# Differential attention as one pipeline over its heads, RWKV blocks inverted in 64x64 halves, and inverse roots by logarithm and exponential

## The reference, cut to what matters

```python
def _rmsnorm(x, g, eps=NORM_EPS):          # used on x, on the MLA latents, on the output of differential attention
    y = xf * lax.rsqrt(jnp.mean(xf * xf, axis=-1, keepdims=True) + eps)
    return (y * g.astype(jnp.float32)).astype(x.dtype)

def _rwkv7_mix(...):                       # 8 heads of 64
    kk = kk / jnp.maximum(jnp.linalg.norm(kk, axis=-1, keepdims=True), 1e-12)
    def step(state, inp):                  # 1024 steps
        sa = jnp.einsum('bhij,bhj->bhi', state, -kk_t)
        state = (state * w_t[:, :, None, :] + sa[..., None] * b_t[:, :, None, :]
                 + v_t[..., None] * k_t[:, :, None, :])
        return state, jnp.einsum('bhij,bhj->bhi', state, r_t)
    y = ((y - mean) * lax.rsqrt(var + RWKV_GN_EPS)).reshape(B, S, RWKV_DIM) * ln_w + ln_b

def _diff_mix(...):                        # 4 heads, two maps each, Q_BLOCK = 128
    def block(q0, q1, mask):
        logits = jnp.einsum('bhmqd,bhmkd->bhmqk', q[:, :, :, q0:q1], k[:, :, :, :q1]) * scale + bias
        probs = _masked_softmax(logits, mask)
        attn = probs[:, :, 0] - lam_full * probs[:, :, 1]
        return jnp.einsum('bhqk,bhkd->bhqd', attn.astype(v.dtype), v[:, :, :q1])
    o = _rmsnorm(o, subln, eps=1e-5) * (1 - lambda_init)
```

## Time and profile before

| what | value |
|---|---|
| median of 3 runs | 6106.19 us (6104.87 to 6108.89) |
| profiled execution | 6102.16 us, span 6100.4 us |
| PE, DVE, ACT, POOL busy | 85%, 31%, 22%, 10% of the span |
| mean granted clock of TensorE | 0.91 |
| one RWKV pair (the second) | 531.0 to 772.5 us |
| differential attention behind its projections | 2030.7 to 2306.1 us |

### The profile page before, as it was taken

How to read it: one execution, slowest core, us unless ns; L and a number is a source line. 1 busy time by engine, 2 the same in 40 slices (tenths; PEclk the granted TensorE clock), 3 DMA queues, 4 the chain that set the end, 5 groups by cost and what they waited for, 6 DMA issues and landing times. The chain is left out here.

```text
span 6100.4 us, 63978 instructions
## 1 busy us (share of the span) xinstructions
PE 5159.5 (85%) x24753; PEld 2840.6 (47%) x24753; DVE 1895.1 (31%) x3299; ACT 1331.5 (22%) x2074; POOL 616.5 (10%) x419
## 2 busy tenths in 40 slices
PE   6688888898799657799989949787788876999899
PEld 2264756743354344344434414675556642444344
DVE  5343442511640351211110034544423632111101
ACT  2222121211330351122220011223213421222200
POOL 0030220300000001000000010222210001000000
PEclk9898898889899768899999979898889998999999
DMA  3501001010011002111113302101110001111111
GB/s 76 84 6 27 18 20 28 6 47 26 11 36 49 31 31 83 32 38 38 40 47 102 111 11 68 38 5 41 41 39 1 1 21 28 38 38 38 36 38 50
DMA packets 301641, 231.72 MB, mean 38 GB/s; under 512 B 30355, under 2 KB 266695, under 8 KB 301383
## 3 DMA queue, kind: packets, MB, share of 16 engines
q1 hardware_dynamic: 301418, 228.46, 13.4%
HBM read 203.76 MB, written 24.67 MB: 37 GB/s over the span
## 5 line engine op out<-in xcount | busy, mean ns | idle before, releaser
L628 PE MATMUL psum<-ffn_in,up_slots 128*128 128x512 f32 x2816 | 1213.8, 594 | 65.3 <-DMA up_slots<-in_w_up_dram 41.4
L628 PEld LDWEIGHTS psum<-ffn_in,up_slots 128*128 128x128 f32 x2816 | 536.6, 191 | 742.5 <-issue 742.5
L665 DVE SCALAR_TENSOR_TENSOR conv<-u,conv_cols_a,conv 128x1024 f32<-128x1024 f32 x88 | 113.0, 1284 | 984.2 <-ACT conv L647 984.2
L442 PE MATMUL psum<-hidden,w_slots 128*128 128x512 f32 x704 | 305.4, 597 | 16.3 <-DMA w_slots<-in_w_down_dram 16.3
L2268 PE MATMUL psum<-hidden,w_slots 128*128 128x512 f32 x704 | 306.1, 596 | 10.7 <-DMA w_slots<-in_ffn_w_down_dram 10.7
L644 ACT ACTIVATE u<-psum 128x512 f32<-128x512 f32 x176 | 105.2, 598 | 893.4 <-PE psum L628 893.4
L2794 PE MATMUL psum<-h,w_slots 128*128 128x512 f32 (+1 forms) x576 | 225.0, 551 | 45.7 <-issue 43.5
L679 POOL TENSOR_TENSOR hidden<-conv 128x1024 f32 x44 | 103.1, 2342 | 1323.6 <-DVE conv L669 1323.6
L442 PEld LDWEIGHTS psum<-hidden,w_slots 128*128 128x128 f32 x704 | 134.8, 192 | 186.9 <-issue 169.8
L2268 PEld LDWEIGHTS psum<-hidden,w_slots 128*128 128x128 f32 x704 | 133.9, 191 | 177.6 <-issue 166.6
L1556 PE MATMUL psum<-x,w_slots 128*128 128x512 f32 x384 | 175.0, 619 | 34.2 <-issue 23.8
(11 more groups left out here) (559 smaller groups left out, 8178.7 us busy)
## 6 DMA issues: line engine op xcount, KB each, us to landing
mod_slots<-in_w_mod_dram SPq DMA_DIRECT2D x12, 2048.0 KB, 8.8
up_slots<-in_ffn_w_up_dram SPq DMA_DIRECT2D x44, 512.0 KB, 3.9
up_slots<-in_w_up_dram SPq DMA_DIRECT2D x44, 512.0 KB, 4.0
w_slots<-in_w_in_dram SPq DMA_DIRECT2D x38, 512.0 KB, 5.3
w_slots<-in_ffn_w_down_dram SPq DMA_DIRECT2D x8, 1408.0 KB, 12.6
w_slots<-in_w_down_dram SPq DMA_DIRECT2D x8, 1408.0 KB, 6.8
rows_in<-in_x_dram SPq DMA_DIRECT2D x16, 512.0 KB, 3.6
gate_w<-in_w_in_dram SPq DMA_DIRECT2D x16, 512.0 KB, 5.8
```

Of the source, the lines that this page charges most:

```text
L442: last = nc.tensor.matmul(T.ps[2 * s + j][:, :], slots[:, s, k, :], rhs(k)[:, j * HALF:(j + 1) * HALF], start=(k == 0), stop=(k == kt - 1))
L628: last = nc.tensor.matmul(T.ps[b][:, :], slots[:, q, k, :], h[:, k, j * HALF:(j + 1) * HALF], start=(k == 0), stop=(k == KD - 1))
L665: nc.vector.scalar_tensor_tensor(out=conv[:, q, :], in0=u[:, q, first:first + S], scalar=conv_w[first][:, bass.ds(col, 1)], in1=conv[:, q, :],
```

## The change

It has five parts. `channel_rms`, `rwkv_prepare` and `rwkv_finish` take the inverse root by Ln and Exp on ScalarE; the epsilons come from a small constant tile. `rwkv_solve` forms the 64x64 chunks alone and calls `invert_halves`. `diff_attention` has no loop stage: one stage runs 32 units (4 heads x 8 tiles), with the normalisation's root once per head and the output turned 11 units later. Its projection loops are written out, the scale is folded into the evictions, and the bias of heads 0 and 1 is loaded there. `turn_tokens` is gone, and GATE_ORDER in block 2 is permuted.

```diff
 def channel_rms
-                act.wait_ge(mean_made, len(halves))
-                nc.scalar.activation(inv[:, :], inv[:, :], ACT.Sqrt).then_inc(root_made, 1)
+                act.wait_ge(summed, kd)
+                nc.scalar.activation(inv[:, :], T.psum[:, 0:n], ACT.Ln, scale=1.0 / (kd * P), bias=T.eps[:, 0:1]).then_inc(log_made, 1)
+                act.wait_ge(log_made, 1)
+                nc.scalar.activation(inv[:, :], inv[:, :], ACT.Exp, scale=-0.5).then_inc(inverse_made, 1)
...
-                    nc.vector.tensor_scalar(inv[:, c:c + w], T.ps[j][:, 0:w], 1.0 / (kd * P), eps,
-                                            ALU.mult, ALU.add).then_inc(mean_made, 1)
-                dve.wait_ge(root_made, 1)
-                nc.vector.reciprocal(inv[:, :], inv[:, :]).then_inc(inverse_made, 1)
 def rwkv_solve
+                    for t in (2 * g, 2 * g + 1):
+                        for c, rows in enumerate(CHUNKS):
+                            toks = slice(t * P + c * CH, t * P + (c + 1) * CH)
+                            for e, ch in enumerate(CHUNKS):
+                                for kind in range(2):
+                                    at = ((t % 2) * 2 + kind) * P
+                                    last = nc.tensor.matmul(T.ps[2 * (g % 2) + e][rows, at:at + P], bk[ch, kind, toks], kr[ch, t, :, rows],
+                                                            start=True, stop=True)
+                                low = nc.tensor.matmul(T.ps[4 + e][rows, t * CH:(t + 1) * CH], kr[ch, t, 0, rows], bk[ch, 0, toks],
+                                                       start=True, stop=True)
...
-        invert_blocks(nc, T, ltrb, inv, inv_t, xs, lm, [(4 * g, 4, 0) for g in range(GROUPS)], range(1, 6),
-                      lambda k, d: T.join_mask[:, k:k + 1, :])
+        invert_halves(nc, T, lt, inv, inv_t, xs, lm, groups, range(1, 6), lambda k, d: T.half_joins[:, k:k + 1, :])
 def diff_attention, projection stage
+                    load_bias(sp, 0, bias_loaded)
+                    load_bias(sp, 1, bias_loaded)
+                    sp.wait_ge(bias_loaded, 16 * 2 * NT)
 def diff_attention, the one stage; TensorE
+                    for u in range(U + LAG):
+                        if u < U:
...
+                                pe.wait_ge(logits_made, 2 * u)
+                            for c in range(0, w, HALF):
+                                wd = min(HALF, w - c)
                                 for m in range(2):
...
+                                    last = nc.tensor.matmul(T.ps[2 * m + c // HALF][:, 0:wd], qk[rows, n, t * P:(t + 1) * P],
+                                                            qk[rows, DH + n, c:c + wd], start=True, stop=True)
...
+                        if 1 <= u <= U:
+                            v = u - 1
+                            pe.wait_ge(mixed, v + 1)
...
+                        if u >= LAG:
+                            d = u - LAG
+                            pe.wait_ge(scaled, d + 1)
+                            if d >= 1:
+                                pe.wait_ge(out_made, d)
+                            nc.tensor.transpose(T.ps[7][:, 0:P], o_rows[:, d % (2 * NT), :], T.ident[:, :]).then_inc(back_turned, 1)
```

More of the change, by code:

```diff
@@ L1177, in diff_attention @@
     scale = float(DQK ** -0.5)
+    U, LAG = DH * NT, 11
+    units = [(n, t) for n in range(DH) for t in range(NT)]
+    groups, first_group = [], []
+    for n, t in units:
+        first_group.append(len(groups))
+        groups += [(k0, min(4, t + 1 - k0)) for k0 in range(0, t + 1, 4)]
+    first_group.append(len(groups))
+    by_dve = [(g - max(f for f in first_group if f <= g)) % 2 for g in range(len(groups))]
+    copied = lambda n, side: by_dve[:n].count(side)
     with ExitStack() as keep:
@@ L1226, in _ @@
                     nc.scalar.activation(neg_lam[:, 0:2], neg_lam[:, 0:2], ACT.Exp).then_inc(exps_made, 1)
[L1227 removed]
+                    for i in range(steps):
                         for s in range(2):
                             act.wait_ge(made[2 * s], i + 1)
[L1230 to L1231 removed]
+                            nc.scalar.activation(qk[:, 2 * i + s, 0:HALF], T.ps[2 * s][:, :], ACT.Copy,
+                                                 scale=scale if 2 * i + s < DH else 1.0).then_inc(kept[2 * s], 1)
                 @block.vector
                 def _(dve):
[L1235 removed]
                     dve.wait_ge(lam_loaded, 16)
@@ new lines, in _ @@
+                for e in range(2):
+                    nc.vector.tensor_tensor(inv[:, e * NT:(e + 1) * NT, :], T.ps[4 + e][:, :].rearrange("p (q n) -> p q n", q=NT),
+                                            T.half_low.to_broadcast([P, NT, CH]), ALU.mult).then_inc(low_masked, 1)
+            @block.scalar
+            def _(act):
+                for i, (g, e) in enumerate(steps):
+                    act.wait_ge(masked, i + 1)
+                    u0 = e * NT + 2 * g
+                    nc.scalar.activation(lt[:, u0:u0 + 2, :], pairs[:, u0:u0 + 2, 0, 0, :], ACT.Copy).then_inc(lt_kept, 1)
@@ new lines, in _ @@
+                for t in range(NT):
+                    for e, ch in enumerate(heads):
+                        for c, rows in enumerate(CHUNKS):
+                            mm = nc.tensor.matmul(T.ps[4 + c][ch, t * CH:(t + 1) * CH], tm[rows, 0, t, ch], inv_t[rows, e * NT + t, :],
+                                                  start=True, stop=True)
+                mm.then_inc(w_made, 1)
+                for t in range(NT):
+                    if t % 4 == 0:
+                        pe.wait_ge(av_kept, t // 4 + 1)
+                    for e, ch in enumerate(heads):
+                        for rows in CHUNKS:
+                            mm = nc.tensor.matmul(T.ps[2 + t // 4][rows, (t % 4) * P + ch.start:(t % 4) * P + ch.stop],
+                                                  inv_t[rows, e * NT + t, :], av[rows, t, ch], start=True, stop=True)
+                    if t % 4 == 3:
@@ L2530 @@
 GUNITS = DIRS * NTC
-GATE_ORDER = (7, 2, 1, 0, 5, 3, 6, 4)
+GATE_ORDER = (0, 6, 7, 3, 4, 1, 2, 5)
 GROWS = 36
@@ L3176, in constants @@
         "ident": np.eye(P), "ones": np.ones((P, P)), "head_ones": same,
-        "chunk_masks": np.concatenate([same & (s < t), same & (s <= t)], 1),
-        "join6": np.concatenate([join(2 ** k) for k in range(6)], 1), "low": join(1).T, "not_first": first,
+        "half_pair": np.concatenate([halves(s < t), halves(s <= t)], 1), "half_low": halves(join(1).T), "not_first": first,
         "causal": np.where(s >= t, 0, -1e30), "rope": rope,
@@ L3182, in constants @@
         "half_swap": (s ^ 32) == t, "head_sel": s // 64 == np.arange(2)[None],
+        "eps": np.array([[1e-6, 64e-5]]) * np.ones((P, 1)),
         "pair_sums": np.arange(P)[:, None] % 32 == np.arange(2)[None],
```

549 lines of the change are left out of this document (244 added, 305 removed).

## The result

The changed kernel takes 5861.83 us (median of 4 runs, 5856.53 to 5867.02) against 6105.53 for the kernel before on the same chip: ratio 0.9602, 95% interval 0.9585 to 0.9618. The direction was right. The forecast of 5917 was 55 us too slow and its range ended 6 us above the measured time.

A forecast was written before the change was run, and what follows sets the result against it. Barrier-ended stages add up: TensorE bounds RWKV's inversion, waits bound attention, a VectorE reciprocal the norms. Savings 38 (norms) + 107 (RWKV) + 45 (attention) - 1 = 189 off 6106 gave 5917 us, range 5868 to 5966.

The forecast's parts named there:

- Norms: Seven channel norms: VectorE starts 3.6 us after the logarithm, 5.4 us saved each, 38 us in all.
- The exposed second table load: Channel norms: the exponential's table load of 1.28 us stands in the chain, the logarithm's own load costs nothing.
- Hidden edits: RWKV preparation and finish: removed reciprocals were covered by TensorE's gate products, so 0 saved (preparation bounds 0 and -2 us).
- Inversion: RWKV inversion: 896 records at 0.029 us, 26.0, plus 6.3 overhead make 32.3 us; 22 saved per pair.
- Attention: Differential attention, 275.4 us to 230 (bounds 203 and 256), 45 saved; a new loop of waits through VectorE's scaling.
- Stage before the inversion: RWKV: TensorE's 17.1 us become 13.7 by partial overlap; 2 us saved per pair (bounds 0 and 4).
- Products behind: RWKV, behind the inversion: 6.8 us of full-rate products become 5.6; 3 us saved per pair (bounds 2 and 7).
- Rival 4: Written-out attention rounds each meet an instruction refill, 205 us: attention 435, kernel 6122; chance 0.03.
- Rival 1: TensorE's slow clock rules the attention loop: 256 us or a little over instead of 230, kernel 5945; chance 0.2.
- Rival 2: 64x64 halves don't reach TensorE's rate: inversion 38 us instead of 32, 3 lost before it, kernel 5953; chance 0.12.
- Rival 3: Better clock all along: attention 205, stage behind inversion 4 better, next stages' first waits gone, kernel 5876; chance 0.15.
- Rivals 4 and 5: Rival 5: attention rounds overlap no better than before, attention stays at 275, kernel 5962; chance 0.08.

The follow-up runs named there:

- the filler: Four unused transposes on TensorE behind the last product of RWKV's inversion, added to the kernel before: 6077.28 us (one run, 6101.93 beside it).
- the reorderings: Kernel after with attention's output turned back one round later (5830.18 us), with scores ahead of the transposes (5810.22), or with both (5808.87).
- the run with row halves apart: Kernel after with products before and behind RWKV's inversion reordered so that neighbours read the same 64 rows, except where a group ends: 5898.94 us (one run).

## Why the prediction was wrong, and where it was right

**The direction and five of the steps held.** Norms: 3.52 us behind the logarithm (3.6), 4.1 to 5.5 saved in each where I had 5.4. The exposed second table load was right and shows in the rows of after (1.28 us at 2339.51). The rule of the Trainium skill that I weighed against it (ScalarE: Activation LUTs, "Table sets: the hidden batching unit") has one load for the two functions, which the trace does not bear out. Hidden edits: 0, shown by putting the roots back. Inversion: 29.25 us of records at a clock of 0.92 where 26.0 were counted at 1.00, but less overhead, 30.6 against 32.3; two errors that cancel in part. Attention: 232.7 against 230, with the chain as written, a round of 10.5 from seven to eight blocks, no head's start of 10 us left, and its wait for the scaling shown by taking it away.

**Stage before the inversion: "the last 64 of each head (low part) overlap with the other head's first product".** This is the first step that failed, 4.7 us a pair. All products of the two heads ran together: 9.26 us, not 13.7. What ends the stage then is POOL: with its last two passes on VectorE the stage is 1.3 us shorter.

**Products behind: "6.8 us of products at full rate, 14.2 seen because of the clock, become 5.6. At the same clock, saved 3."** Two errors. At full clock the stage before the change needs 9.35 us of TensorE and is 10.0 long (run with the four transposes), and after the change 5.12 and 6.1 to 6.7. So the blocks are worth 3.3 to 3.9 us, not 1.2: a product of 64 columns with full weights costs as much as one of 128. The other 4 or so are the clock's: it costs 4.8 us before (14.8 - 10.0) and 0.4 to 1.0 after. I had taken the clock of before as given, though it was half only until 463 us. The whole saved 7.7 us a pair against the 3 of the sum, and passed even the bound of 7, which left out the first error. What makes the low stretch shorter after the change is not settled; the filler shows only what goes ahead of its beginning.

**Gated delta's preparation: no term.** Nothing in the prediction priced where unchanged code comes to lie. Rival 4 spoke of instruction supply, but only inside the new stage and only as a loss. The page of before had the place: 43.5 us of "issue" ahead of this line's matmuls, the most of any line of matmuls on it. The stage lost 14.8 us without an edit. Eight unused transposes take 13.3 off it in the kernel before, so the new count of instructions is enough for nearly all; which of the change's parts shifts it in the full change is not separated. That this term fell on the side of the gain is luck: with two instructions more the kernel before was 3 us slower there.

**The rivals.** Rival 1 (slow clock rules the loop) fell: attention took 232.7 us, not 256, and with the reorderings the waits went and the clock rose. The slow clock had a share, 1.8 us in the largest round's scores. Its argument from the 36.6 us of the first two heads "whatever the clock" was none: both heads had the same granted clock, 0.69. Rival 2 fell with the inversion at 30.6 us, not 38. Rival 3 had the right place in one of its three terms, behind the inversion, and the right price there; its others, attention at 205 and the next stages' first waits, didn't come. Rivals 4 and 5 didn't come. The range was too narrow because it held bounds for the clock and for known edits, and none for the error of a count by columns, which failed in two stages in the same direction, nor for unchanged code.

## What to carry to other kernels

A loop of waits is found by writing down each engine's list and asking which instruction stands ahead of the one that frees the next; here moving TensorE's scores ahead of the transposes was worth 52 us, about a third of what the whole RWKV change brought. Before a stage is priced by columns, divide busy time by records at clock 1.00, one group of products at a time: in one stage they ran from 0.059 to 0.118 us. When unchanged code moves by some us, look for "issue" gaps at the top of its loop, on every engine and ahead of the stage as well as in it, and shift the instructions ahead of it by a few before anything else is blamed.

## What the runs showed of the hardware

- A stop of 2.2 to 3.3 us inside a loop body moved by exactly the two TensorE instructions added ahead of the loop (then 3.9 to 4.4 us, two records sooner) and went away with four and with eight. In another kernel VectorE too came late at the top of the same loop, 4.1 to 4.2 us instead of 1.5.
- TensorE's clock fell to 1.2 GHz at the start of the products behind RWKV's inversion in all 20 such stages of the five kernels with the old order and 1.66 or 1.67 us of idle time ahead; in none of the 8 stages with the idle time cut to 1.22 to 1.24 us. In the new order, with 1.73 us of idle time, it fell in 23 of 28, and in two of four in the run with row halves apart, so the idle time is not all that decides.
- 64x64 f32 products in different quarters of the array ran together: 0.029 us a record with the same rows and alternating outputs, closer still with all four quarters in turn (0.018); in one quarter they followed at 0.052. With alternating rows and three in a row in one quarter, 17.07 us of products took 9.26.
- Products with 128x128 weights and 64 columns took 0.115 to 0.118 us a record at full clock, no less than the 0.109 of 128 columns in the old inversion. Products of 128 columns with weights 64 wide and alternating output halves took 0.059.
